# The rotation of the differential heads: from a permutation product on TensorE to eight 32-partition products on VectorE

## The chip, the cores and the metric

The kernel runs on one core of a Trainium2 chip. The metric is device time in microseconds (us) of one execution. The engines are called PE (TensorE, matrix products), DVE (VectorE), ACT (ScalarE), POOL (GpSimd) and SP (the engine that here only issues transfers).

## What is computed

The kernel computes a first block (RWKV mixer, convolution, feed-forward network) and a second block with two attention layers over 512 tokens and 256 context tokens. Only the second attention layer, with differential heads, is touched. It has 8 heads. Each has two queries and two keys of 64 dimensions, laid out on 128 partitions (dimension on the partition, token along the free axis). Queries and keys of the 512 tokens are rotated:

```python
def apply_rope(x, cos, sin):
    half = x.shape[-1] // 2
    x1 = x[..., :half].astype(jnp.float32)
    x2 = x[..., half:].astype(jnp.float32)
    return jnp.concatenate([x1 * cos - x2 * sin, x2 * cos + x1 * sin], axis=-1).astype(x.dtype)
...
        q = q.reshape(bsz, n, 2 * B_HEADS, B_HEAD)
        k = k.reshape(bsz, n, 2 * B_HEADS, B_HEAD)
        if rope:
            q = apply_rope(q, cos, sin)
            k = apply_rope(k, cos, sin)
```

So with 64 dimensions a half is 32: partitions 0 to 31 exchange with 32 to 63, and 64 to 95 with 96 to 127. Afterwards come the two softmaxes, their difference, the product with the values, a norm and a gate.

## The kernel before

Every engine has its own program, written out by hand; they meet at counting semaphores. The differential layer is a loop over heads. In iteration h, PE computes the projection of head h + 1 (four parts q, k, gate, v of eight chunks each, so 32 chunks c = 0 to 31, function `diff_chunk`, matrix products on L1390, L1391 and L1393) and puts the attention of head h between the chunks: scores u = 0 to 7 (`diff_scores`, L1425 and L1426) ahead of chunks 0, 3, ... 21, the transposes of the probabilities (`diff_turn`, L1433) ahead of chunks 8, 14, 20, 28, and the product with the values (`diff_values`, L1445) ahead of chunks 10, 16, 22, 30. PE executes its queue in order, so a wait in one of these holds everything behind it.

The rotation of head h + 1 in iteration h:

- ACT copies q and k from PSUM into `dq` (L1983) and `dk` (L1987).
- PE, ahead of chunk 19, multiplies both with a permutation matrix that also carries the signs (`diff_rotate`, L1400 and L1401), into PSUM.
- DVE multiplies the result with the sines (`read_rotated`, L2753 and L2754, into `dtq` and `dtk`), later `dq` and `dk` with the cosines (L2757, L2758) and adds (L2760, L2761), in `rope_sum`.
- ACT rounds to the high parts (`high_own`, `high_other`, L2007 to L2014), DVE takes the low parts (`low_parts`, L2765 to L2768). The scores of head h + 1 need both.

The order of DVE's queue in the last third of an iteration is fixed:

```python
            top(h, 6)
            read_rotated(h + 1)
            copy_turn(h, 2)
            rope_sum(h + 1)
            top(h, 7)
            mix(h, 3)
            out(h, 2)
            copy_turn(h, 3)
            low_parts(h + 1)
            out(h, 3)
```

`top` is the row maximum of a score (L2772), `mix` combines the two softmaxes (L2777 to L2781), `copy_turn(h, 2)` (L2787) copies half of the transposed probabilities out of PSUM, and `diff_values(h, 2)` on PE waits for it.

POOL splits each block of weights (1 MB, sixteen 128x128 tiles) into a high and a low part, eight instructions of 128x512 a block (L648 high, L639 low), two blocks a head. It may start on a block as soon as PE has finished with the buffer: after chunk 15 (the k part) and after chunk 31 (the v part). For head 0 the rotation stands outside the loop, between the chunks of head 0, and nothing of another head surrounds it; POOL also splits a block there.

Of the kernel before, what the change touches and what calls it, by code (L numbers as in the profile page):

```python
# [19 lines left out]
ALU = mybir.AluOpType  # L20
# [3 lines left out]
P = 128  # L24
T = 512
# [89 lines left out]
def build(nc, x_t, ctx_t, stream, ada_w, vectors, squares, level_masks, scan_mask, ropes, lora_w, gate_w,  # L115
# [10 lines left out]
    def fixed(name, shape, dt=F32, size=4):  # L126
        n = size
        for s in shape[1:]:
            n *= s
        t = at(name, shape, dt, place[0])  # L130
        place[0] += (n + 31) // 32 * 32
        return t
# [5 lines left out]
    sq_c = fixed("sq_c", [P, 8, P])  # L138
# [24 lines left out]
    sq = reg("sq", [P, KT, T], 16)  # L163
# [50 lines left out]
    pairs = [es.enter_context(nc.psum_tensor(f"banks{2 * i}{2 * i + 1}", [P, 2, 512], F32)) for i in range(4)]  # L214
# [6 lines left out]
    def sem(name):  # L221
        return es.enter_context(nc.semaphore(name))
# [42 lines left out]
    lora_in, lora_full, lora_evac = sem("lora_in"), sem("lora_full"), sem("lora_evac")  # L265
    chunk_end, exps_in, exps_done = sem("chunk_end"), sem("exps_in"), sem("exps_done")
    kk_raw, kk_sq, kk_sum, kk_max, kk_root = (sem(n) for n in ("kk_raw", "kk_sq", "kk_sum", "kk_max", "kk_root"))
# [109 lines left out]
    rope = at("rope", [P, 2, T], F32, tmp_at)  # L377
# [94 lines left out]
    dq = reg("dq", [P, T], 115)  # L472
    dk = reg("dk", [P, TA], 117)
# [4 lines left out]
    dtq = reg("dtq", [P, T], 135)  # L478
    dtk = at("dtk", [P, T], F32, tmp_at + 4 * KB)
# [11 lines left out]


    q_full = Later(lora_in, 2)
    rot_full = Later(lora_full, 12)
    gate_full = Later(lora_evac, 12)
    vt_full = Later(chunk_end, 1)
    q_evac = Later(exps_in, 2)
    k_evac = Later(exps_done, 4)
    gate_evac = Later(kk_raw, 4)
    v_evac = Later(kk_sq, 4)  # L500
    vt_evac = Later(kk_sum, 4)
    rot_read = Later(kk_max, 4)
    roped = Later(kk_root, 4)
    qk_high = Later(bonus_in, 4)
    qk_low = Later(bonus_sum, 4)
# [13 lines left out]
    X_PAIR, TURN, G_BANK, O_BANK = 1, (4, 5), 6, 7  # L519
# [199 lines left out]
    def _(pe):  # L719
        pe.wait_ge(one_done, 1)  # L720
        for k in range(KT):
            pe.wait_ge(sq_full, k + 1)
            for j in range(4):
                mm = pe.matmul(banks[7][:, j:j + 1], sq[:, k, P * j:P * j + P], der[:, ONE:ONE + 1], start=(k == 0 and j == 0),
                               stop=(k == KT - 1 and j == 3), skip_group_check=True)
# [199 lines left out]
        for n in range(NCH):  # L925
            tt, r = n // 2, slice(64 * (n % 2), 64 * (n % 2) + 64)
# [21 lines left out]
            for h in range(8):  # L948
                c, hr = h // 2, slice(64 * (h % 2), 64 * (h % 2) + 64)
# [10 lines left out]
            if n == 4:  # L960
                for c in range(CT):
                    pe.wait_ge(cln_sq, c + 1)
                    for j in range(4):
                        mm = pe.matmul(banks[5][32 * j:32 * j + 32, 0:P], ones[:, 0:32], csq[:, c, P * j:P * j + P], start=(c == 0),
                                       stop=(c == CT - 1))
# [44 lines left out]
        for c in range(CT):  # L1010
            rows = slice(32 * c, 32 * c + 32)
# [38 lines left out]
        with pe.Fori(0, 2) as i:  # L1050
            for u in range(6):
                s = half_of(STREAM["down"] + u)
                for t in range(TILES):
# [7 lines left out]
                    b = banks[4 + m]  # L1061
# [306 lines left out]
        def diff_chunk(h, part, k):  # L1368

            A, B = half_of(DIFF_A[h]), half_of(DIFF_A[h] + 1)  # L1370
            w, tile, wide_out = {"q": (A, k, False), "k": (A, KT + k, True), "gate": (B, k, False), "v": (B, KT + k, True)}[part]
            if k == 0:
                if part == "q":
                    pe.wait_ge(split_full, DIFF_A[h] + 1)
                    if h:
                        pe.wait_ge(*gate_evac.at(h))
                elif part == "k":
                    pe.wait_ge(*(vt_evac.at(h) if h else x_centred.at(KT)))
                elif part == "gate":
                    pe.wait_ge(split_full, DIFF_A[h] + 2)  # L1380
                    pe.wait_ge(*q_evac.at(h + 1))
                elif part == "v":
                    pe.wait_ge(*rot_read.at(h + 1))
            if h == 0 and part == "q":
                pe.wait_ge(mh_ready, KT + k + 1)
            hi, lo = w_hi[:, w, tile, :], w_lo[:, w, tile, :]
            own = key_pair(h) if part == "k" else X_PAIR
            spans = ((pairs[own][:, 0, :], 0, T), (pairs[own][:, 1, 0:C], T, TA)) if wide_out else ((banks[G_BANK][:, :], 0, T),)
            for out, a, b in spans:
                pe.matmul(out, hi, h2_hi[:, k, a:b], start=(k == 0), stop=False)  # L1390
                pe.matmul(out, hi, h2_lo[:, k, a:b], start=False, stop=False)  # L1391
            for out, a, b in spans:
                mm = pe.matmul(out, lo, h2_hi[:, k, a:b], start=False, stop=(k == KT - 1))  # L1393
            if k == KT - 1:
                mm.then_inc({"q": q_full.sem, "k": block_done, "gate": gate_full.sem, "v": block_done}[part], 1)

        def diff_rotate(h):
            pe.wait_ge(*q_evac.at(h + 1))
            pe.wait_ge(*k_evac.at(h + 1))
            pe.matmul(pairs[X_PAIR][:, 0, :], sq_c[:, 3, :], dq[:, :], start=True, stop=True)  # L1400
            pe.matmul(pairs[X_PAIR][:, 1, :], sq_c[:, 3, :], dk[:, 0:T], start=True, stop=True).then_inc(rot_full.sem, 1)  # L1401

        def diff_turn_v(h):
            pe.wait_ge(*v_evac.at(h + 1))
# [43 lines left out]
        PARTS = [(part, k) for part in ("q", "k", "gate", "v") for k in range(KT)]  # L1448
        TURN_AT, VALUES_AT = (8, 14, 20, 28), (10, 16, 22, 30)
        for c, (part, k) in enumerate([(part, k) for k in range(KT) for part in ("q", "k")] + PARTS[2 * KT:]):  # L1450
            if c == 19:
                diff_rotate(0)
            diff_chunk(0, part, k)
        for h in range(B_HEADS - 1):
            for c, (part, k) in enumerate(PARTS):
                if c % 3 == 0 and c < 24:
                    diff_scores(h, c // 3)
                if c == 2:
                    diff_turn_v(h)
                if c == 19:  # L1460
                    diff_rotate(h + 1)
                if c in TURN_AT:
                    diff_turn(h, TURN_AT.index(c))
                if c in VALUES_AT:
                    diff_values(h, VALUES_AT.index(c))
                diff_chunk(h + 1, part, k)
        h = B_HEADS - 1
# [660 lines left out]
    def _(dve):  # L2128
        chain = Chain(dve, dve_step)
# [196 lines left out]
        for n in range(NCH):  # L2326
            tt, r = n // 2, slice(64 * (n % 2), 64 * (n % 2) + 64)
# [113 lines left out]
        with conv.loop(N_UP // 2, 4) as i:  # L2441
            for u in range(2):
                s = half_of(STREAM["up"] + u)
                j = 2 * i + u
                for g, buf in enumerate((yg, yu)):
                    b = banks[2 * s + g]
# [45 lines left out]
        for e in range(2):  # L2492
            r, s = rope_rows(e), swap_rows(e)
# [4 lines left out]
        for e in range(2):  # L2498
            r = rope_rows(e)
# [24 lines left out]
        for e in range(2):  # L2524
            r = rope_rows(e)
# [61 lines left out]
        for e in range(2):  # L2587
            r = rope_rows(e)
# [160 lines left out]
        low_rows, high_rows = slice(0, 64), slice(64, 128)  # L2749

        def read_rotated(h):
            dve.wait_ge(*rot_full.at(h + 1))
            dve.tensor_tensor(dtq[:, :], pairs[X_PAIR][:, 0, :], rope[:, 1, :], ALU.mult)  # L2753
            dve.tensor_tensor(dtk[:, :], pairs[X_PAIR][:, 1, :], rope[:, 1, :], ALU.mult).then_inc(rot_read.sem, 1)  # L2754

        def rope_sum(h):
            dve.tensor_tensor(dq[:, :], dq[:, :], rope[:, 0, :], ALU.mult)  # L2757
            chain.link(dve.tensor_tensor(dk[:, 0:T], dk[:, 0:T], rope[:, 0, :], ALU.mult))  # L2758
            dve.wait_ge(*rot_read.at(h + 1))
            dve.tensor_tensor(dq[:, :], dq[:, :], dtq[:, :], ALU.add)  # L2760
            dve.tensor_tensor(dk[:, 0:T], dk[:, 0:T], dtk[:, :], ALU.add).then_inc(roped.sem, 1)  # L2761

# [65 lines left out]
        h = B_HEADS - 1  # L2828
# [38 lines left out]
        for t in range(4):  # L2867
            o = O_tok[:, t, P * h:P * h + P]
# [190 lines left out]
def constants():  # L3059

    j, t = np.meshgrid(np.arange(P), np.arange(P), indexing="ij")
    same = (j // CHUNK) == (t // CHUNK)
    sq = np.zeros((P, 9, P), np.float32)
    sq[:, 8] = (np.arange(P)[:, None] % 32 // 16 == np.arange(P)[None, :] // 64) / 16.0
    sq[:, 0] = j == t
    sq[:, 1] = 1
    sq[:, 2] = same
    sq[:, 4] = same & (j < t)
    sq[:, 5] = same & (j <= t)

    def rotation(rows, half):

        r = np.zeros((P, P), np.float32)
        for start in rows:
            for i in range(half):
                r[start + half + i, start + i] = -1
                r[start + i, start + half + i] = 1
        return r
    sq[:, 3] = rotation([0, 64], 32)
    lv = np.zeros((P, 12, P), np.float32)  # L3080
    for n in range(6):
        s = 1 << n
        low = (j // (2 * s) == t // (2 * s)) & (j % (2 * s) >= s) & (t % (2 * s) < s)
        lv[:, n] = low
        lv[:, 6 + n] = low.T
    scan = np.ones((P, T), np.float32)
    scan[:, ::CHUNK] = 0

    def angles(dim):
        n = dim // 4  # L3090
        inv = (np.float32(10000.0) ** (-np.arange(n, dtype=np.float32) / np.float32(n))).astype(np.float32)
        row, c = np.repeat(np.arange(T // 64, dtype=np.float32), 64), np.tile(np.arange(64, dtype=np.float32), T // 64)
        return np.concatenate([row[:, None] * inv, c[:, None] * inv], axis=-1).T
    ropes = np.zeros((2, P, 2, T), np.float32)
    a = angles(32)
    for o in (32, 48, 64, 80):
        ropes[0, o:o + 16, 0] = np.cos(a)
    for o in (0, 96):
        ropes[0, o:o + 16, 1], ropes[0, o + 16:o + 32, 1] = -np.sin(a), np.sin(a)
    b = angles(64)  # L3100
    for o in range(0, P, 32):
        ropes[1, o:o + 32, 0], ropes[1, o:o + 32, 1] = np.cos(b), np.sin(b)
    return {"squares": sq, "level_masks": lv, "scan_mask": scan, "ropes": ropes}


# [15 lines left out]
```

## Time and profile before

| quantity | value |
|---|---|
| median of 3 runs | 1777.9 us (1777.76 to 1782.23) |
| profiled execution, first to last instruction (its span) | 1776.4 us |
| PE busy | 1697.5 us (96%) |
| DVE busy | 1014.9 us (57%) |
| ACT busy | 763.0 us (43%) |
| POOL busy | 954.4 us (54%) |

For the profiled execution only the span is recorded; the median of the runs is 1.5 us above it. Busy time is what an engine's instructions took; a duration of a DVE or POOL instruction includes time in which it could not proceed. A row of the timeline gives the start, the duration, the engine and line, output<-inputs, the shapes, and in brackets the idle time of the engine before it with what ended it.

### The profile page before, as it was taken

Reading aid. Unit: us, or ns where it says so; the run is one execution under the profiler, and the core shown is the slowest. Engines: PE = TensorE matmul, PEld = TensorE weight load, DVE = VectorE, ACT = ScalarE, POOL = GpSimd, SP = SyncE. Lnnn points to the kernel's source line nnn. Section 1 sums busy time; section 2 is a strip of 40 time slices with the busy share of each in tenths; the row PEclk is TensorE's granted clock in tenths of the full one; section 3 lists DMA queues with packets and bytes.
Section 4 is the critical chain, followed back from the end, with each engine's and each line's share of the span. In section 5 each row is a group of like instructions: output and inputs, shape, how many; then the busy total and the mean of one; then the engine's idle time right before and its main releaser. Section 6 shows DMA issues by size and latency. Waiting matters only on the chain.

```text
span 1776.4 us, 26816 instructions
## 1 busy us (share of the span) xinstructions
PE 1697.5 (96%) x10602; PEld 1393.1 (78%) x10602; DVE 1014.9 (57%) x1276; ACT 763.0 (43%) x1261; POOL 954.4 (54%) x758
## 2 busy tenths in 40 slices
PE   8999999989799999999998999999989999999987
PEld 7677999867488888888787777776877888888765
DVE  4697544575655555201455666667485666666575
ACT  4553767422333333101433565567134444444572
POOL 4443777767099999999356022224554444444062
PEclk9999999989899999999999999999999999999998
DMA  5221000233022222424112000001331111111211
GB/s 191 72 95 48 2 1 2 97 145 157 33 75 101 102 100 94 166 101 170 50 48 72 25 24 1 25 0 57 110 155 48 48 47 44 45 45 46 88 68 48
DMA packets 18870, 126.38 MB, mean 71 GB/s; under 512 B 2096, under 2 KB 2352, under 8 KB 4304
## 3 DMA queue, kind: packets, MB, share of 16 engines
q1 hardware_dynamic: 18624, 124.41, 19.1%
q8 instruction: 75, 1.23, 0.3%
q10 hardware_dynamic: 144, 0.52, 0.1%
q14 instruction: 27, 0.22, 0.0%
HBM read 122.83 MB, written 2.10 MB: 70 GB/s over the span
## 4 chain that ended last, share of the span: by engine, by line
PE 51%; issue 19%; POOL 16%; DVE 9%; ACT 3%; DMA 0%; POOLq 0%; ACTq 0%; DVEq 0%; SPq 0%
POOL w_hi L648 8%; PE banks L1233 5%; POOL cacc L670 4%; PE banks L1212 4%; POOL w_lo L639 3%; PE banks L1390 3%; PE banks L1393 3%; PE banks L1391 3%; PE banks L1095 3%; PE banks L1100 3%; PE banks L1096 3%; PE banks L751 2%; PE banks L1445 2%; PE banks L752 2%; PE banks L753 2%
## 5 line engine op out<-in xcount | busy, mean ns | idle before, releaser
L648 POOL TENSOR_TENSOR w_hi<-raw,der 128x512 fp32r<-128x512 f32 x296 | 341.0, 1162 | 455.8 <-PE banks L1393 184.9
L639 POOL TENSOR_TENSOR w_lo<-raw,w_hi 128x512 fp32r<-128x512 f32 x336 | 468.9, 1408 | 65.9 <-ACT w_hi L1536 65.9
L751 PE MATMUL banks<-h_hi,w_hi 128*128 128x512 f32 x496 | 198.7, 401 | 5.6 <-DVE h_lo L2368 5.3
L752 PE MATMUL banks<-h_lo,w_hi 128*128 128x512 f32 x496 | 194.4, 392 | 0.0
L753 PE MATMUL banks<-h_hi,w_lo 128*128 128x512 f32 x496 | 194.2, 392 | 0.0
L1390 PE MATMUL banks<-h_hi,w_hi 128*128 128x512 f32 (+1 forms) x384 | 146.8, 382 | 0.1
L1391 PE MATMUL banks<-h_lo,w_hi 128*128 128x512 f32 (+1 forms) x384 | 131.5, 358 | 0.0
L2019 ACT ACTIVATE dP<-banks,der 128x768 f32<-128x768 f32 x64 | 57.7, 902 | 159.9 <-DVE der L2772 159.9
L751 PEld LDWEIGHTS banks<-h_hi,w_hi 128*128 128x128 f32 x496 | 93.6, 189 | 35.1 <-issue 12.7
L1393 PE MATMUL banks<-h_hi,w_lo 128*128 128x512 f32 (+1 forms) x384 | 116.5, 358 | 0.0
L698 POOL TENSOR_TENSOR Of<-Of,Ls 128x768 f32<-128x768 f32 x8 | 14.7, 1833 | 186.7 <-DVE Ls L2574 186.7
L752 PEld LDWEIGHTS banks<-h_lo,w_hi 128*128 128x128 f32 x496 | 93.8, 189 | 19.8 <-issue 1.4
L753 PEld LDWEIGHTS banks<-h_hi,w_lo 128*128 128x128 f32 x496 | 93.8, 189 | 19.5
L2772 DVE TENSOR_REDUCE der<-banks 128x1 f32<-128x768 f32 x64 | 60.8, 953 | 70.0 <-PE banks L1426 69.9
L1233 PE MATMUL banks<-Pf,V 128*128 128x512 f32 x192 | 99.2, 598 | 0.3 <-issue 0.3
L1095 PE MATMUL banks<-h_hi,w_hi 128*128 128x512 f32 (+1 forms) x256 | 92.6, 362 | 4.6 <-DVE h_lo L2471 1.8
L2563 DVE TENSOR_REDUCE nmr<-banks 128x1 fp32r<-128x768 f32 x64 | 60.5, 945 | 59.7 <-PE banks L1183 58.9
L670 POOL TENSOR_TENSOR cacc<-glu_s,cacc 128x512 f32<-128x512 f32 x48 | 60.3, 1278 | 63.7 <-ACT glu_s L1634 63.7
L1872 ACT ACTIVATE Pf<-banks 128x512 f32<-128x512 f32 x112 | 66.6, 595 | 62.8 <-PE banks L1212 60.8
L1096 PE MATMUL banks<-h_lo,w_hi 128*128 128x512 f32 (+1 forms) x256 | 86.1, 353 | 0.0
L1390 PEld LDWEIGHTS banks<-h_hi,w_hi 128*128 128x128 f32 x384 | 72.8, 190 | 16.4 <-issue 1.9
L1391 PEld LDWEIGHTS banks<-h_lo,w_hi 128*128 128x128 f32 x384 | 73.1, 190 | 10.3 <-issue 1.9
(491 smaller groups left out, 4152.5 us busy)
## 6 DMA issues: line engine op xcount, KB each, us to landing
raw<-in_stream SPq DMA_DIRECT2D x84, 1024.0 KB, 4.8
ada_raw<-in_ada_w SPq DMA_DIRECT2D x18, 1024.0 KB, 6.9
raw<-in_ada_w SPq DMA_DIRECT2D x4, 1024.0 KB, 4.8
xT<-in_x_t SPq DMA_DIRECT2D x2, 1024.0 KB, 6.1
xT<-in_x_t SPq DMA_DIRECT2D x1, 2048.0 KB, 7.9
ada_end<-in_ada_w SPq DMA_DIRECT2D x2, 1024.0 KB, 5.8
out_t<-z SPq DMA_DIRECT2D x8, 256.0 KB, 2.1
ctxT<-in_ctx_t SPq DMA_DIRECT2D x1, 1024.0 KB, 6.8
```

The costliest lines, as they stand in the source:

```text
L639: return pool.tensor_tensor(lo[:, h, part(i), :], raw_tiles(half)[:, part(i), :], hi[:, h, part(i), :], ALU.subtract)
L648: pool.tensor_tensor(hi[:, h, part(i), :], raw_tiles(half)[:, part(i), :], one, ALU.mult).then_inc(hi_done, 1)
L670: pool.tensor_tensor(cacc[:, j, :], tap_out[i % 4], cacc[:, j, :], ALU.add).then_inc(conv_done, 1)
L751: pe.matmul(banks[b][:, :], hi, tile(rhs_hi, k), start=(at_k == 0), stop=False)
L752: pe.matmul(banks[b][:, :], hi, tile(rhs_lo, k), start=False, stop=False)
L753: mm = pe.matmul(banks[b][:, :], lo, tile(rhs_hi, k), start=False, stop=(at_k == KT - 1))
L1095: pe.matmul(out, hi, cols(rhs_hi, k0 + k, a, b), start=(k == 0), stop=False)
L1096: pe.matmul(out, hi, cols(rhs_lo, k0 + k, a, b), start=False, stop=False)
L1233: mm = pe.matmul(pairs[1][:, 0, :], v[:, j, :], Pf[:, i % 4, :], start=(j == 0), stop=(j == 5), skip_group_check=True)
L1390: pe.matmul(out, hi, h2_hi[:, k, a:b], start=(k == 0), stop=False)
L1391: pe.matmul(out, hi, h2_lo[:, k, a:b], start=False, stop=False)
L1393: mm = pe.matmul(out, lo, h2_hi[:, k, a:b], start=False, stop=(k == KT - 1))
```

## The change

PE's permutation product goes away, with its semaphores. DVE reads the neighbouring half straight from `dq` and `dk` in SBUF: for each 32 partitions one product, input and sines at partitions r + 32, output at r, and the reverse; four for q and four for k, eight a head. The sign moves into the table of sines. `rope_sum` now begins with a wait until all eight are finished, and the v part of the projection (chunk 24) waits for the copy of k instead of the reading of the rotated product.

```diff
@@ PE @@
                 elif part == "v":
-                    pe.wait_ge(*rot_read.at(h + 1))
+                    pe.wait_ge(*k_evac.at(h + 1))
...
-        def diff_rotate(h):
-            pe.wait_ge(*q_evac.at(h + 1))
-            pe.wait_ge(*k_evac.at(h + 1))
-            pe.matmul(pairs[X_PAIR][:, 0, :], sq_c[:, 3, :], dq[:, :], start=True, stop=True)
-            pe.matmul(pairs[X_PAIR][:, 1, :], sq_c[:, 3, :], dk[:, 0:T], start=True, stop=True).then_inc(rot_full.sem, 1)
...
-            if c == 19:
-                diff_rotate(0)
...
-                if c == 19:
-                    diff_rotate(h + 1)
@@ DVE @@
         def read_rotated(h):
-            dve.wait_ge(*rot_full.at(h + 1))
-            dve.tensor_tensor(dtq[:, :], pairs[X_PAIR][:, 0, :], rope[:, 1, :], ALU.mult)
-            dve.tensor_tensor(dtk[:, :], pairs[X_PAIR][:, 1, :], rope[:, 1, :], ALU.mult).then_inc(rot_read.sem, 1)
+            for src, dst, done in ((dq, dtq, q_evac), (dk, dtk, k_evac)):
+                dve.wait_ge(*done.at(h + 1))
+                for r in range(0, P, 64):
+                    low, high = slice(r, r + 32), slice(r + 32, r + 64)
+                    chain.mark(dve.tensor_tensor(dst[low, :], src[high, 0:T], rope[high, 1, :], ALU.mult))
+                    chain.mark(dve.tensor_tensor(dst[high, :], src[low, 0:T], rope[low, 1, :], ALU.mult))
 
         def rope_sum(h):
+            chain.wait()
             dve.tensor_tensor(dq[:, :], dq[:, :], rope[:, 0, :], ALU.mult)
             chain.link(dve.tensor_tensor(dk[:, 0:T], dk[:, 0:T], rope[:, 0, :], ALU.mult))
-            dve.wait_ge(*rot_read.at(h + 1))
@@ the table of sines @@
-        ropes[1, o:o + 32, 0], ropes[1, o:o + 32, 1] = np.cos(b), np.sin(b)
+        ropes[1, o:o + 32, 0], ropes[1, o:o + 32, 1] = np.cos(b), -np.sin(b) if o % 64 else np.sin(b)
```

## Rows read from the trace of the kernel before

**Rows 1.** The page's first line.

```profile
span 1776.4 us, 26816 instructions
```

**Rows 2.** Busy time by engine in one iteration: us, busy by engine (instructions), granted clock.

```profile
1475.70:1520.40 44.70, 44.55 (x260) 37.72 (x259) 27.92 (x39) 18.97 (x40) 19.87 (x17) 1.00 0.14 48
```

**Rows 3.** Timeline of PE in one iteration, from chunk 19 on.

```profile
1478.14 1.02 PE L1400 MATMUL banks<-dq,sq_c 128*128 128x512 f32 x2
...
1480.09 0.39 PE L1391 MATMUL banks<-h_lo,w_hi 128*128 128x512 f32 x1
1480.32 0.39 PE L1393 MATMUL banks<-h_hi,w_lo 128*128 128x512 f32 x1
...
1483.29 1.50 PE L1445 MATMUL banks<-dV,dPT 128*128 128x128 f32 x12
...
1496.41 0.40 PE L1425 MATMUL banks<-KK,QQ 128*128 128x512 f32 x1
```

**Rows 4.** Timeline of DVE over the same rotation.

```profile
1478.56 0.94 DVE L2772 TENSOR_REDUCE der<-banks 128x1 f32<-128x768 f32 x1
1480.06 0.69 DVE L2753 TENSOR_TENSOR dtq<-banks,rope 128x512 f32<-128x512 f32 x1 [0.56 <-PE banks L1401]
...
1481.27 0.55 DVE L2787 COPY dPT<-banks 128x384 f32<-128x384 f32 x1
1481.73 1.58 DVE L2757 TENSOR_TENSOR dq<-dq,rope 128x512 f32<-128x512 f32 x1
1483.23 1.75 DVE L2758 TENSOR_TENSOR dk<-dk,rope 128x512 f32<-128x512 f32 x1
```

**Rows 5.** Timeline of POOL over the same rotation.

```profile
1479.23 1.27 POOL L639 TENSOR_TENSOR w_lo<-raw,w_hi 128x512 fp32r<-128x512 f32 x1
1480.46 1.04 POOL L648 TENSOR_TENSOR w_hi<-raw,der 128x512 fp32r<-128x512 f32 x1
1481.46 2.98 POOL L639 TENSOR_TENSOR w_lo<-raw,w_hi 128x512 fp32r<-128x512 f32 x2
```

**Rows 6.** Timeline of DVE: two low parts whose inputs and outputs start at other partitions.

```profile
1491.60 0.69 DVE L2765 TENSOR_TENSOR QQ<-dq,QQ 64x512 fp32r<-64x512 f32 x1 [0.28 <-ACT KK L2010]
1492.30 0.69 DVE L2766 TENSOR_TENSOR QQ<-dq,QQ 64x512 fp32r<-64x512 f32 x1
```

**Rows 7.** One line of the first attention layer: duration ns least/median/greatest, first and last start.

```profile
L2547 DVE TENSOR_TENSOR qf<-qf,otmp x16: 681/896/1336, 944.1 to 1203.0; 32x512 f32<-32x512 f32 x16
```

**Rows 8.** Timeline of the last iteration (rotation of head 7).

```profile
1656.53 0.96 DVE L2772 TENSOR_REDUCE der<-banks 128x1 f32<-128x768 f32 x1 [0.69 <-PE banks L1426]
...
1660.16 0.55 DVE L2787 COPY dPT<-banks 128x384 f32<-128x384 f32 x1
...
1662.19 1.50 PE L1445 MATMUL banks<-dV,dPT 128*128 128x128 f32 x12
...
1686.67 2.04 POOL L648 TENSOR_TENSOR w_hi<-raw,der 128x512 fp32r<-128x512 f32 x2 [46.13 <-DMA raw<-in_stream]
```

**Rows 9.** Timeline of the rotation of head 0, ahead of the loop.

```profile
1341.87 0.70 DVE L2795 MEMSET KL<- 64x768 f32 x1 [0.20 <-issue]
...
1342.91 2.04 POOL L648 TENSOR_TENSOR w_hi<-raw,der 128x512 fp32r<-128x512 f32 x2 [27.18 <-PE banks L1393]
...
1352.04 1.78 DVE L2761 TENSOR_TENSOR dk<-dk,dtk 128x512 f32<-128x512 f32 x1
...
1356.86 0.69 DVE L2765 TENSOR_TENSOR QQ<-dq,QQ 64x512 fp32r<-64x512 f32 x1 [3.05 <-ACT KK L2010]
...
1358.58 3.25 POOL L648 TENSOR_TENSOR w_hi<-raw,der 128x512 fp32r<-128x512 f32 x2 [5.32 <-PE banks L1393]
...
1361.18 0.47 PE L1425 MATMUL banks<-KK,QQ 128*128 128x512 f32 x1 [2.69 <-DVE KL L2768]
```

**Rows 10.** Two stretches of reduced granted clock: us, busy by engine, granted clock.

```profile
454.70:461.50 6.80, 4.61 (x6) 1.80 (x7) 6.80 (x12) 2.52 (x4) 0.00 (x0) 0.50 0.00 0
1362.60:1366.00 3.40, 3.40 (x12) 2.81 (x12) 0.52 (x1) 1.48 (x3) 3.40 (x4) 0.50 0.02 5
```

More of the change, by code:

```diff
@@ L493, in build @@
     q_full = Later(lora_in, 2)
-    rot_full = Later(lora_full, 12)
     gate_full = Later(lora_evac, 12)
@@ L501, in build @@
     vt_evac = Later(kk_sum, 4)
-    rot_read = Later(kk_max, 4)
     roped = Later(kk_root, 4)
@@ L3069, in constants @@
     sq[:, 5] = same & (j <= t)
[L3071 to L3079, printed above, removed]
     lv = np.zeros((P, 12, P), np.float32)
```

## The prediction

> **What bounds the kernel now.** I read the page first for the span [rows 1], then the busy time of one iteration of the head loop. An iteration takes 44.70 us and PE is busy for 44.55 of it, at full granted clock [rows 2]. So in the loop PE has practically no slack: what is taken off PE shortens it, and any wait on PE that wasn't there lengthens it. DVE is busy for 27.92 us and looks idle enough to take more work. But that is an average; the order of DVE's queue is fixed, so I read the timelines of PE, DVE and POOL side by side around the rotation. There the reader is to see three things: the copy L2787 stands directly behind the two products to be replaced, PE's product with the values follows it closely (copy finished at 1481.82, used at 1483.29), and POOL is splitting a block at that moment, while DVE's two SBUF products L2757 and L2758 take 1.58 and 1.75 us [rows 3 to 5].
>
> **What is removed from PE.** L1400 starts at 1478.14 where chunk 19 would start, and the second product of that chunk, L1391, starts at 1480.09. Consecutive products of a chunk are 0.23 us apart (1480.09, 1480.32). Without the rotation L1391 would start at 1478.37, so it costs 1480.09 - 1478.37 = 1.72 us a head, 13.8 us for 8 heads [rows 3]. This is the whole possible gain. The changed wait of chunk 24 costs nothing: the copy of k that it waits for lies ahead of the rotation already.
>
> **What is added to DVE.** Two products reading PSUM, 0.61 us each from start to start (1480.06 to 1481.27 for both, rows 4), make way for eight of 32 partitions reading SBUF twice. The trace of before has no such instruction, but close ones. With two SBUF inputs, 32x512, L2547 took 0.68 us at least and 1.34 at most, so 32 rows are neither cheaper than 128 nor free of the lengthening [rows 7]. When inputs and outputs change their first partition from one instruction to the next, starts are 0.70 us apart (1491.60, 1492.30) [rows 6]; the new ones change it every time, so I take 0.70 undisturbed. The lower bound is 0.61 (the PSUM products).
>
> Beside POOL they are longer. POOL's pair of L639 at 1481.46 takes 2.98 us where two alone take 2 x 1.27 = 2.54, and DVE's L2758 ends at 1484.98, 0.54 us after the pair (1484.44) [rows 4, 5]. Read together: the two engines take turns, one instruction each; DVE's ends about 0.55 us after POOL's, and each one put between lengthens POOL by 0.44 us.
>
> The Trainium skill (SBUF — State Buffer, "SBUF: two separate sides") says why: DVE instructions with two SBUF inputs and POOL instructions lock a common port pair for a whole instruction, and reading PSUM avoids that. The trace agrees (1.58 and 1.75 us here, 0.69 for L2753). By that rule alone the sum below would be the same; it speaks against the change, which turns PSUM readers into SBUF readers.
>
> **One iteration, h = 0 to 5.** `top(h, 6)` ends at 1479.50 [rows 4]. POOL is inside L639 until 1480.50 and has three instructions left (1.04, 1.27, 1.27) [rows 5].
>
> - Product 1 ends at 1480.50 + 0.55 = 1481.05.
> - POOL ends its next ones at 1480.46 + 0.44 + 1.04 = 1481.94, then + 0.44 + 1.27 = 1483.65, then 1485.36; products 2, 3 and 4 end at 1482.49, 1484.20 and 1485.91.
> - POOL is through; products 5 to 8 take 4 x 0.70: 1488.71. Then the copy, 0.55: 1489.3.
>
> PE can take up the product with the values at 1489.3. It would want it at 1483.29 - 1.72 = 1481.57, so it stands for 7.7 us, and against before it is 6.0 us late. Everything behind it in PE's queue is late too: ten chunks and the scores of the next head, 13.12 us later (1496.41 [rows 3]), now at 1502.4. Does a second wait follow? The low parts end near 1494.9 now (1491.60, two at 0.70 and two half again as long), 13.1 us after the copy, with 1.9 us of POOL's turns in it that are gone by then; that gives 1489.3 + 11.2 = 1500.5, before 1502.4. So it doesn't, by 1.9 us. POOL's own block ends about 1 us later, and before its next block it has more than ten us of rest (two blocks keep it busy 19.87 of 44.70 us, rows 2). 6 x 6.0 = 36 us.
>
> **The clock.** After a stall PE runs at half clock (1.2 for 2.4 GHz) for a while. After the 2.69 us stall at 1358.5 [rows 9] it was 0.50 for 3.40 us, all busy: 1.7 us lost. In the first layers a longer stall, ended at about 456.9, had 6.80 us of 0.50 around it, 4.61 of them busy: 2.3 us lost [rows 10]. For a stall of 7.7 us I take 2.0: 6 x 2.0 = 12 us. With none of it, 0; with all of 6.8 us busy, 3.4 a head.
>
> The Trainium skill (TensorE: Matmul & The Clock Gate, "Why this matters for your kernels") wants no gap above about 3 us to stay at full clock. Here 2.69 us was enough, so the row decides; by the page only the last head below could come out otherwise, by 1.7 us.
>
> **The last iteration, head 7.** POOL has nothing to do (idle for 46 us until 1686.67) [rows 8]. `top` ends at 1657.49, eight products make 1663.09, the copy 1663.65, against 1662.19 for the use before: 1.5 us late, a stall of 3.2, and 1.7 for the clock: 3.2 us.
>
> **Head 0.** Product 1 can start behind L2795 at 1342.6 and end at 1343.3. POOL then begins its block; products 2 to 8 take turns with seven of its eight instructions (7.97 us alone, and 6 x 0.44): the eighth ends near 1354.4, the sums near 1358.3 instead of 1353.82. ACT's 3.04 us of rounding bring the low parts to 1361.4 instead of 1356.86. PE is finished with its chunks 1.72 us earlier and releases POOL's next block (1358.58 before, about 1356.9 now), so all four low parts now take turns with it, some 1.0 us more for each of three or four: PE goes on near 1369 instead of 1361.18 [rows 9]. 8 us; bounds -5 (no turns at all, no stall) and 11.
>
> **Sum.** 36 + 12 + 3.2 + 8 = 59 us on the profiled execution's 1776.4, so 1835.6; the median lies 1.5 us above that span, so 1837 us, 3.3% slower.
>
> **Rivals.**
>
> 1. *The stall as above, but the clock isn't lowered, or far less.* For: PE has been dense for 30 us before it. Against: all of rows 10. 1837 - 12 - 2 = 1823. Chance 0.15.
> 2. *No turns with POOL*: 32 partitions don't wait, or POOL yields. Each copy then ends at 1479.50 + 8 x 0.70 + 0.55 = 1485.65, 2.4 us late, plus 1.7 for the clock: 7 x 4 = 28, less 5 for head 0: about 1800. With 0.61 for 0.70 and no clock loss, 1785. Against: 1.34 us of a 32x512 row [rows 7]. Chance 0.08.
> 3. *A second wait behind the first.* If the four sums or ACT's rounding come later than worked out, the 1.9 us of margin ahead of the next head's scores is used up; with the longer clock loss (3.4) as well, 10 to 11 us a head: 1777.9 + 6 x 10.5 + 3 + 11 = 1855. Chance 0.11.
> 4. *Not slower.* PE's 1.72 us is kept. This needs the copy L2787 by 1481.5, so eight products within 1.5 us of 1479.5, 0.19 us each, where no row is under 0.61; or DVE's `top(h, 6)` more than 4 us earlier. It decides at a product price of 0.19 us. Then 1777.9 - 13.8 = 1764. Chance 0.02, and 0.01 for within 0.3% (half of the gain eaten by head 0).
>
> My forecast has 0.63. The range reaches from near the second rival to the third: 1805 to 1852 us. Within 0.3% (5 us) is about what a measurement of this kernel can't tell from no change. Faster 0.02, same 0.01, slower 0.97.
>
> **What the profile will show.** Eight 32x512 products a head: the first four 1.4 to 1.8 us apart, the rest 0.70; L2787 of each third turn ending about 9.8 us after `top(h, 6)`; an idle time of 7 to 8 us on PE before L1445, released by DVE's copy, six times, and about 3 us a seventh time; after it a granted clock of 0.50 for some 3.4 us or more; an iteration of 52 to 53 us in place of 44.70; POOL's L639 in that stretch longer by 0.44. Before L1425 of head 0 PE idles some 12 us instead of 2.69. The prediction is wrong if the new products don't take turns with POOL, if PE's product with the values doesn't wait, or if DVE's order lets the copy go first.

## The result and the profile after

The changed kernel takes 1840.4 us (median of 4 runs, 1836.8 to 1848.7), the kernel before 1780.1 us in the same comparison: ratio 1.0349, 95% interval 1.0329 to 1.0370. It is slower by 3.5%; 1837 us and 3.3% were forecast. The profiled execution has a span of 1838.9 us against 1776.4.

The page's first lines for the changed kernel: span, busy time by engine, and the granted clock in 40 slices.

```profile
span 1838.9 us, 26784 instructions
...
PE 1708.5 (93%) x10570; PEld 1403.6 (76%) x10570; DVE 1064.3 (58%) x1324; ACT 763.4 (42%) x1261; POOL 963.6 (52%) x758
...
PEclk9999999999999999999999999999889899898998
```

PE's count is 32 lower than before (10602): each of the 16 products taken out is recorded as two instructions. Yet PE's busy time went up by 11 us: less work at a lower clock. Where, the last third of the slices (`PEclk`, tenths of the full clock) shows.

The timeline of DVE over one rotation in the loop of the changed kernel answers to [rows 4]:

```profile
1504.58 0.94 DVE L2763 TENSOR_REDUCE der<-banks 128x1 f32<-128x768 f32 x1
1505.55 1.53 DVE L2744 TENSOR_TENSOR dtq<-dq,rope 32x512 f32<-32x512 f32 x1
1507.11 1.42 DVE L2745 TENSOR_TENSOR dtq<-dq,rope 32x512 f32<-32x512 f32 x1
1508.56 1.64 DVE L2744 TENSOR_TENSOR dtq<-dq,rope 32x512 f32<-32x512 f32 x1
1510.23 1.64 DVE L2745 TENSOR_TENSOR dtq<-dq,rope 32x512 f32<-32x512 f32 x1
1511.90 0.68 DVE L2744 TENSOR_TENSOR dtk<-dk,rope 32x512 f32<-32x512 f32 x1
1512.61 0.68 DVE L2745 TENSOR_TENSOR dtk<-dk,rope 32x512 f32<-32x512 f32 x1
1513.33 0.69 DVE L2744 TENSOR_TENSOR dtk<-dk,rope 32x512 f32<-32x512 f32 x1
1514.04 0.68 DVE L2745 TENSOR_TENSOR dtk<-dk,rope 32x512 f32<-32x512 f32 x1
1514.76 0.56 DVE L2778 COPY dPT<-banks 128x384 f32<-128x384 f32 x1
```

The first four are lengthened, the other four are 0.71 us apart, and the copy ends at 1515.32, 9.8 us after `top(h, 6)` (1505.52). POOL's timeline beside it answers to [rows 5], and PE's to [rows 3]:

```profile
1505.26 1.28 POOL L637 TENSOR_TENSOR w_lo<-raw,w_hi 128x512 fp32r<-128x512 f32 x1
1506.50 1.49 POOL L646 TENSOR_TENSOR w_hi<-raw,der 128x512 fp32r<-128x512 f32 x1
1507.95 3.38 POOL L637 TENSOR_TENSOR w_lo<-raw,w_hi 128x512 fp32r<-128x512 f32 x2
```

```profile
1506.60 0.50 PE L1417 MATMUL banks<-KK,QQ 128*128 128x512 f32 x1 [0.22 <-ACT dP L2007]
...
1515.37 2.93 PE L1437 MATMUL banks<-dV,dPT 128*128 128x128 f32 x12 [7.09 <-DVE dPT L2778]
```

POOL's block ends at 1511.33, which is when the products become short. PE stood still for 7.09 us for the copy, and the twelve products with the values then took 2.93 us instead of 1.50 [rows 3], at a granted clock of 0.50. The waits of the whole stage name two new ones on PE and nothing else of size (us in total, times, longest):

```profile
PE banks L1437 <- DVE dPT L2778: 45.8, 7, 7.1
...
PE banks L1417 <- DVE KL L2759: 11.2, 1, 11.2
```

Two windows of the changed kernel (busy by engine, then the granted clock), each from the third low part of one head to that of the next, answer to [rows 2]:

```profile
1474.02:1526.47 52.45, 44.94 (x256) 38.28 (x255) 33.82 (x45) 19.00 (x40) 20.75 (x16) 0.93 0.11 41
1526.47:1579.86 53.39, 45.91 (x256) 39.01 (x255) 33.80 (x44) 19.00 (x40) 20.74 (x16) 0.90 0.11 40
```

Measured between the same marks (the third low part of a head, L2767 before, L2758 after), the 62.5 us between the two spans lie here: 1.8 us ahead of the rotation of head 0 (L2795 at 1341.87, its counterpart at 1343.67; nothing there was changed); 5.8 us in the rotation of head 0; 54.5 us from head 0's mark to head 7's (313.4 to 367.9 us); 0.4 us behind it.

### The profile page after: what moved, and what is told of

It is laid out like the page before. It is cut to its first block, busy times and chain, and to the rows that moved or that the text cites. A ratio compares the mean times of both kernels' runs of the same rounds, so it can differ in the third digit from the quotient of the medians.

```text
span 1838.9 us, 26784 instructions
## 1 busy us (share of the span) xinstructions
PE 1708.5 (93%) x10570; PEld 1403.6 (76%) x10570; DVE 1064.3 (58%) x1324; ACT 763.4 (42%) x1261; POOL 963.6 (52%) x758
## 4 chain that ended last, share of the span: by engine, by line
PE 47%; issue 19%; POOL 16%; DVE 14%; ACT 3%; DMA 0%; POOLq 0%; ACTq 0%; DVEq 0%; SPq 0%
POOL w_hi L646 8%; PE banks L1231 4%; POOL cacc L668 4%; PE banks L1210 3%; POOL w_lo L637 3%; PE banks L1093 3%; PE banks L1388 3%; PE banks L1391 3%; PE banks L1389 3%; PE banks L1098 3%; PE banks L1094 3%; PE banks L1437 2%; PE banks L749 2%; PE banks L750 2%; PE banks L751 2%
## 5 line engine op out<-in xcount | busy, mean ns | idle before, releaser
L646 POOL TENSOR_TENSOR w_hi<-raw,der 128x512 fp32r<-128x512 f32 x296 | 345.2, 1177 | 511.0 <-PE banks L1391 236.2
L637 POOL TENSOR_TENSOR w_lo<-raw,w_hi 128x512 fp32r<-128x512 f32 x336 | 474.5, 1425 | 67.0 <-ACT w_hi L1524 67.0
L1389 PE MATMUL banks<-h_lo,w_hi 128*128 128x512 f32 (+1 forms) x384 | 133.9, 363 | 0.0
L750 PEld LDWEIGHTS banks<-h_lo,w_hi 128*128 128x128 f32 x496 | 93.7, 189 | 19.9 <-issue 1.4
L1437 PE MATMUL banks<-dV,dPT 128*128 128x128 f32 x384 | 58.5, 311 | 50.3 <-DVE dPT L2778 47.4
L1437 PEld LDWEIGHTS banks<-dV,dPT 128*128 128x128 f32 x384 | 54.2, 222 | 54.8 <-DVE dPT L2778 50.8
L668 POOL TENSOR_TENSOR cacc<-glu_s,cacc 128x512 f32<-128x512 f32 x48 | 60.3, 1278 | 63.9 <-ACT glu_s L1622 63.9
```

The lines of the kernel that those rows point to most:

```text
L637: return pool.tensor_tensor(lo[:, h, part(i), :], raw_tiles(half)[:, part(i), :], hi[:, h, part(i), :], ALU.subtract)
L646: pool.tensor_tensor(hi[:, h, part(i), :], raw_tiles(half)[:, part(i), :], one, ALU.mult).then_inc(hi_done, 1)
L668: pool.tensor_tensor(cacc[:, j, :], tap_out[i % 4], cacc[:, j, :], ALU.add).then_inc(conv_done, 1)
L750: pe.matmul(banks[b][:, :], hi, tile(rhs_lo, k), start=False, stop=False)
L1437: mm = pe.matmul(banks[O_BANK][:, 0:P], dPT[:, kt, :], dV[:, kt, :], start=(kt == 0), stop=(kt == 5))
```

## The experiments

All were compared with the kernel before in runs on the same chip. The first five change the changed kernel in one point each.

**PE's permutation kept.** Its result is read by nobody.

```diff
...
+            if c == 19:
+                diff_rotate(0)
...
+                if c == 19:
+                    diff_rotate(h + 1)
...
         def rope_sum(h):
             chain.wait()
+            dve.wait_ge(*rot_full.at(h + 1))
```

> The changed kernel, with the permutation products of PE put back (their result is read by nobody; the sums wait for them). Theory (the loop is set by DVE's eight products ahead of the copy, PE's 1.72 us a head merely shortens work that then stands still): the iterations of the loop keep their 52.9 us, PE's stall before the product with the values falls from 7.1 to about 5.4 us, and the time is that of the changed kernel within 4 us (about 1840). Rival (the gain of 13.8 us is real and only outweighed by a loss elsewhere): the time rises by 10 to 14 us, to about 1852.

Measured: 1842.3 us, ratio 1.0335 (1.0301 to 1.0370); the changed kernel's is 1.0349, so no difference. One iteration, to be held against the second window above:

```profile
1475.19:1528.68 53.49, 47.42 (x260) 39.89 (x259) 33.81 (x44) 19.12 (x40) 20.77 (x16) 0.94 0.11 40
```

PE is busy for 1.5 us more in an iteration of the same length (53.49 and 53.39), and the stall is shorter:

```profile
1516.51 2.93 PE L1444 MATMUL banks<-dV,dPT 128*128 128x128 f32 x12 [5.90 <-DVE dPT L2790]
```

5.90 instead of 7.09 us, where about 5.4 had been expected; the 0.22 us of wait ahead of a score, seen in the changed kernel, are gone as well. What was taken off PE only made it wait longer.

**The copy first.**

```diff
+            copy_turn(h, 2)
             read_rotated(h + 1)
-            copy_turn(h, 2)
             rope_sum(h + 1)
```

> The changed kernel with one line moved: the copy of the transposed probabilities (third turn) stands ahead of the eight products on DVE. Theory (a wait on the order of DVE's queue): the stall of 7.1 us before the product with the values goes away, but the eight products now delay the last score's maximum and with it the fourth turn: PE idles 5 to 6.5 us there, an iteration takes 50 to 52 us, total about 1825 to 1832. Rival (only the copy mattered): no new stall, iterations of 43 us, total about 1773.

Measured: 1830.2 us, ratio 1.0264 (1.0234 to 1.0295). The stall moved, as the theory has it:

```profile
1520.11 1.54 PE L1425 MATMUL banks<-sq_c,Pd 128*128 128x128 f32 x6 [5.67 <-DVE Pd L2772]
```

PE now stands still for 5.67 us ahead of the fourth turn, because the combination L2772 is behind `top(h, 7)`, which is behind the products. Iterations take 51.2 to 51.7 us but for the first (52.6) and the last. Moving one instruction out of the way isn't enough: 9 us of work in a queue delays whatever comes next in it.

**POOL nearly idle.** POOL splits 8 of the 128 columns of each tile for heads 1 to 7 (high and low parts), so these are computed with mostly old weights.

```diff
...
+            cols = slice(0, 8) if light else slice(0, P)
...
-                pool.tensor_tensor(hi[:, h, part(i), :], raw_tiles(half)[:, part(i), :], one, ALU.mult).then_inc(hi_done, 1)
+                pool.tensor_tensor(hi[:, h, part(i), cols], raw_tiles(half)[:, part(i), cols], one[:, :, cols], ALU.mult).then_inc(hi_done, 1)
```

> The changed kernel, in which POOL splits only 8 of 128 columns of each tile for the weights of heads 1 to 7, so that it takes little time (those heads are computed with old weights). Theory (the first four products of an iteration cost 1.5 us instead of 0.70 because they take turns with POOL): all eight products 0.68 to 0.72 us apart, the stall before the product with the values 3.2 us as in the last iteration, head 0 without its long wait, total about 1795 (-45 against the changed kernel). Rival (32-partition products are dear for a reason of their own, such as the starting partitions): the first four stay at 1.4 to 1.7 us, total within 10 us of 1840.

Measured: 1798.9 us, ratio 1.0087 (1.0053 to 1.0122). The first of each two q products in the whole run (least, median, greatest duration in ns), and PE's waits for the copy:

```profile
L2746 DVE TENSOR_TENSOR dtq<-dq,rope x16: 680/684/687, 1349.6 to 1677.0; 32x512 f32<-32x512 f32 x16
...
PE banks L1439 <- DVE dPT L2780: 24.3, 9, 3.2
```

In the changed kernel the same product (there L2744) goes from 680 to 1642 ns with a median of 1528. The same instruction at the same partitions is short once POOL is out of the way, so neither the 32 partitions nor the starting partitions lengthen it. The stall is 3.2 us seven times, head 0 has almost none (0.8 us), an iteration takes 47.5 us. Of the 60 us, some 42 go with POOL's work, and 17 remain: eight products in front of the copy are too many even at 0.71 us each.

**PE kept at work.** 26 products that nobody reads fill the stall.

```diff
+            if qt == 2 and h < B_HEADS - 1:
+                pe.wait_ge(*o_done.at(n))
+                for _ in range(26):
+                    pe.matmul(banks[O_BANK][:, :], w_hi[:, half_of(DIFF_A[h + 1] + 1), 0, :], h2_hi[:, 0, 0:T], start=True, stop=True)
             pe.wait_ge(*eva_done.at(n + 1))
```

> The changed kernel with 26 products of 128x512 put on PE ahead of the wait of the third product with the values (six us of work that nobody reads, in the place of the 7.1 us stall). Theory (the stall of 7.1 us costs a further 2 us a head because PE then runs at 1.2 GHz): granted clock 1.00 through the loop, iterations of 50.7 to 51.3 us instead of 52.9, total 1825 to 1830. Rival (the clock is not what makes the iterations longer than 50.7 us): total unchanged or higher, 1840 to 1845.

Measured: 1827.3 us, ratio 1.0268 (1.0237 to 1.0300): 13 us less than the changed kernel, with more work. One iteration, and PE across the filled stall:

```profile
1467.12:1518.07 50.95, 49.34 (x282) 41.66 (x281) 33.89 (x45) 18.88 (x40) 20.82 (x16) 1.00 0.12 42
```

```profile
1501.19 6.09 PE L1436 MATMUL banks<-h_hi,w_hi 128*128 128x512 f32 x26
1508.53 1.60 PE L1441 MATMUL banks<-dV,dPT 128*128 128x128 f32 x12 [1.25 <-DVE dPT L2782]
```

Full clock, 50.9 us against a mean of 53.0 in the changed kernel (the five iterations between the first and the last): the lowered clock costs 2.1 us an iteration. From head 0's mark to head 7's the profile is 11.4 us shorter (356.5 for 367.9 us); the last iteration is 0.8 us longer, because there the 26 products take longer than the stall that they fill.

**Two products instead of eight.** The same tiles in SBUF, each partition with itself; the halves are not exchanged.

```diff
-                for r in range(0, P, 64):
-                    low, high = slice(r, r + 32), slice(r + 32, r + 64)
-                    chain.mark(dve.tensor_tensor(dst[low, :], src[high, 0:T], rope[high, 1, :], ALU.mult))
-                    chain.mark(dve.tensor_tensor(dst[high, :], src[low, 0:T], rope[low, 1, :], ALU.mult))
+                chain.mark(dve.tensor_tensor(dst[:, :], src[:, 0:T], rope[:, 1, :], ALU.mult))
```

> The changed kernel with two products of 128 partitions in the place of the eight of 32, reading the same tiles in SBUF (each partition with itself, so the halves are not exchanged). PE's permutation is gone, DVE has no more instructions than before, only its two inputs are both in SBUF. Theory (each SBUF product beside POOL costs 1.5 instead of 0.61 us): the copy ends 1.3 us later than before, the product with the values is taken up about when it was before, with a stall near 1.5 us, an iteration takes 44.4 to 44.7 us, total within 4 us of before (1778 to 1784). Rival (it is the number of products alone): iterations of 43.0 us, total 13 us under before.

Measured: 1780.1 us, ratio 1.0001 (0.9981 to 1.0022). As many DVE instructions as before, no permutation on PE, and no gain:

```profile
1479.23 1.64 DVE L2742 TENSOR_TENSOR dtq<-dq,rope 128x512 f32<-128x512 f32 x1
1480.80 1.52 DVE L2742 TENSOR_TENSOR dtk<-dk,rope 128x512 f32<-128x512 f32 x1
1482.24 0.54 DVE L2775 COPY dPT<-banks 128x384 f32<-128x384 f32 x1
```

PE stands still for the copy and once more ahead of the fourth turn, and is busy for 43.60 us of an iteration:

```profile
1482.84 1.61 PE L1437 MATMUL banks<-dV,dPT 128*128 128x128 f32 x12 [0.78 <-DVE dPT L2775]
...
1490.46 0.87 PE L1425 MATMUL banks<-sq_c,Pd 128*128 128x128 f32 x6 [0.43 <-DVE Pd L2769]
```

Iterations take 45.19 us, 0.5 above the upper end of what was expected (44.4 to 44.7), although the stall ahead of the product with the values is 0.78 and not 1.5 us. With the number of DVE instructions unchanged, moving their source from PSUM to SBUF at this place gives back all that PE saved.

**The products spread.** All eight are kept. Two of q stand where POOL rests, two more behind `top(h, 4)`, the four of k read the projection in PSUM behind the copy, and `top(h, 7)` goes ahead of the sums. PE's v part waits until k has been read.

```diff
...
             out(h, 0)
+            rotated_q(h + 1, 0)
             top(h, 4)
+            rotated_q(h + 1, 64)
             copy_turn(h, 1)
...
-            read_rotated(h + 1)
             copy_turn(h, 2)
-            rope_sum(h + 1)
+            rotated_k(h + 1)
             top(h, 7)
+            rope_sum(h + 1)
```

> The changed kernel with the same eight products spread: two of q behind the first output of an iteration, two behind the maximum of score 4 (POOL rests there), the four of k read PSUM instead of SBUF and stand behind the copy, and the maximum of score 7 goes ahead of the sums. Theory (the loss is only where the products stand and that they take turns with POOL): no stall on PE in the loop, all eight at 0.70 us, an iteration takes 43.0 us, full clock; head 0 still takes turns with POOL for its q products and costs about 5 us. Total 1768 to 1776, 0.3 to 0.7% under before. Rival (eight products are too many for DVE's queue anywhere): scores wait for ACT or DVE elsewhere and iterations take 45 us or more.

Measured: 1774.4 us against 1781.2, ratio 0.9962 (0.9944 to 0.9981): 0.4% under the kernel before and 3.6% under the changed one. The k products and POOL beside them:

```profile
1482.00 0.68 DVE L2743 TENSOR_TENSOR dtk<-banks,rope 32x512 f32<-32x512 f32 x1
1482.71 0.68 DVE L2744 TENSOR_TENSOR dtk<-banks,rope 32x512 f32<-32x512 f32 x1
```

```profile
1481.24 1.28 POOL L638 TENSOR_TENSOR w_lo<-raw,w_hi 128x512 fp32r<-128x512 f32 x1
1482.48 1.03 POOL L647 TENSOR_TENSOR w_hi<-raw,der 128x512 fp32r<-128x512 f32 x1
```

Neither is lengthened by the other. An iteration takes 43.5 us, not the 43.0 expected; PE is busy for 43.1 of it and waits twice for 0.2 us, for ACT ahead of a score and for DVE ahead of a turn.

**The same with k from SBUF.**

```diff
...
-            chain.mark(rotated(dtk, wide(key_pair(h)), 0))
-            rotated(dtk, wide(key_pair(h)), 64).then_inc(rot_read.sem, 1)
+            chain.mark(rotated(dtk, dk, 0))
+            rotated(dtk, dk, 64).then_inc(rot_read.sem, 1)
```

> As the spread kernel, but the four products of k read SBUF. Theory (only SBUF inputs take turns with POOL): those four take 1.4 to 1.7 us each, the combination ahead of the fourth turn is 2 to 3 us later, PE idles about 2 us ahead of that turn, an iteration takes 45 to 47 us, total 1783 to 1800. Rival (POOL doesn't matter at this place): same as the spread kernel.

Measured: 1791.0 us, ratio 1.0051 (1.0031 to 1.0070). Same place, same shape, same neighbours:

```profile
1491.98 1.06 DVE L2742 TENSOR_TENSOR dtk<-dk,rope 32x512 f32<-32x512 f32 x1
1493.08 1.42 DVE L2743 TENSOR_TENSOR dtk<-dk,rope 32x512 f32<-32x512 f32 x1
1494.53 1.65 DVE L2742 TENSOR_TENSOR dtk<-dk,rope 32x512 f32<-32x512 f32 x1
1496.21 1.67 DVE L2743 TENSOR_TENSOR dtk<-dk,rope 32x512 f32<-32x512 f32 x1
```

Four iterations take 45.5 us and one 47.1 (the first and the last aside); PE waits 1.8 us ahead of the fourth turn in each of the first six. In the long iteration the granted clock fell behind this wait (0.61 over the 4.4 us after it), in the others it stayed at 1.00. In head 0 POOL lengthens seven of the eight products again, and the stall ahead of the first score is 11.2 us; in the spread kernel POOL lengthens three, and the stall is 4.1 us.

This kernel has all eight products of the changed one, all reading SBUF; beside the order of DVE's queue only one wait, of DVE for its own product, is new. So the order alone brings 1840.4 down to 1791.0 us, and the source of k this to 1774.4.

**Head 0 with the permutation.** The spread kernel, but head 0 rotated by PE as before.

```diff
...
+            if c == 19:
+                diff_rotate(0)
...
-        rotated_q(0, 0)
-        rotated_q(0, 64)
-        rotated_k(0)
+        dve.wait_ge(*rot_full.at(1))
+        chain.mark(dve.tensor_tensor(dtq[:, :], pairs[X_PAIR][:, 0, :], rope[:, 1, :], ALU.mult))
+        dve.tensor_tensor(dtk[:, :], pairs[X_PAIR][:, 1, :], rope[:, 1, :], ALU.mult).then_inc(rot_read.sem, 1)
...
+    sq[:, 3] = -1.0 * (j == (t ^ 32))
```

> The spread kernel with head 0 rotated by PE's permutation product as before (both entries of the matrix negative, to go with the new table of sines). Theory (head 0 costs time because nothing hides its products and they take turns with POOL): PE's wait ahead of the first score is 2.7 to 4.5 us as before, iterations 43.0 us, total 1764 to 1769, about 12 us under before and 4 to 7 under the spread kernel. Rival (head 0 costs nothing): the same as the spread kernel.

Measured: 1773.1 us, ratio 0.9962 (0.9943 to 0.9981). Against the spread kernel this is no difference that can be told, though the stall ahead of the first score is 2.7 instead of 4.1 us and the iteration behind it 42.6 instead of 45.7 us. The total lies some 4 us above the 1764 to 1769 expected.

## Why the prediction was right, point by point

- *What is removed* (1.72 us a head). This was somewhat too much. With the permutation kept, PE's busy time in an iteration rises by 1.5 us (45.91 to 47.42) and the time stays, so in the changed kernel the term is worth nothing, as predicted. Where PE sets the pace, in the spread kernels, PE is busy for 1.5 us less than before (43.09 for 44.55) and the iteration is 44.7 - 43.5 = 1.2 us shorter; the difference is two waits of 0.2 us each, where before PE was idle for 0.15 us in all.
- *Eight products, turns with POOL.* 9.8 us from `top(h, 6)` to the end of the copy, forecast 9.8. Products 1 to 4 at 1.4 to 1.7 us, the rest at 0.71. That POOL is the cause is shown twice: by the light POOL (0.68 us throughout) and by the pair of spread kernels, in which the PSUM readers take 0.68 us and the SBUF readers up to 1.67 at the same place. The rule of the Trainium skill (SBUF — State Buffer, "SBUF: two separate sides") about the port pair shared by DVE instructions with two SBUF inputs and POOL agrees in both directions: the inputs' place decides, not the size.
- *The stall.* 7.09 us and 0.22 ahead of a score before it, forecast 7.7; the removal that was put too high is part of the difference. Without the clock's part an iteration is 50.9 - 44.7 = 6.2 us longer (forecast 6.0). No second wait came behind it, as worked out: the low parts end at 1528.38 and the next head's scores start at 1530.13, a margin of 1.75 us for the 1.9 forecast.
- *The clock.* Forecast 2.0 us an iteration, measured 2.1 by keeping PE at work (53.0 against 50.9). The first rival, no loss of clock, is out. But the 2.0 was a choice between rows, and no iteration lost just that: the iterations take 52.4 and 53.4 us in turn, so they lose 1.5 and 2.5 us, and that the mean fits is in part luck. The two kinds differ in how long PE works at 1.2 GHz behind the stall, 3.23 or 5.52 us (busy by engine, then the granted clock; the stalls end at 1515.37 and 1461.88):

```profile
1515.37:1518.60 3.23, 3.23 (x14) 3.13 (x15) 3.19 (x5) 0.00 (x0) 0.00 (x0) 0.50 0.02 8
1461.88:1467.40 5.52, 5.52 (x19) 4.94 (x20) 4.36 (x8) 0.99 (x3) 0.00 (x0) 0.50 0.01 3
```

  The stall of 3.21 us in the last iteration lowered it too:

```profile
1722.59 2.19 PE L1437 MATMUL banks<-dV,dPT 128*128 128x128 f32 x12 [3.21 <-DVE dPT L2778]
```

  The iteration is 3.6 us longer than before (48.05 for 44.49), forecast 3.2.
- *Head 0.* A stall of 11.17 us ahead of the first score, forecast 12 (2.69 before [rows 9]):

```profile
1369.72 0.77 PE L1417 MATMUL banks<-KK,QQ 128*128 128x512 f32 x1 [11.17 <-DVE KL L2759]
```

  PE goes on 8.5 us later than before (1369.72 for 1361.18), 1.8 of which were there already: 6.7 us for the 8 forecast. The miss is in the low parts: the four took 6.0 us instead of 4.1, so 1.9 more, where three to four were forecast. On the other side the clock's part behind the stall was left out of the sum: PE then worked for 5.58 us at half clock, before for 3.40 [rows 10], which makes 1.1 us. The two misses nearly cancel (7.8 for 8), and that is luck.
- *The sum.* 59 us forecast, 62.5 between the two spans, 60.3 between the medians. Of the 62.5, 1.8 lie ahead of anything that was changed. The stretch from mark to mark took 54.5 us more, and 51.2 were forecast for the loop. But head 0's mark stands ahead of the moment at which PE goes on, so 1.0 of head 0's own 6.7 us and its 1.1 us of clock fall into that stretch; the loop itself is then about 52.4, and some 1.2 us short in the forecast.
- *The rivals.* No turns with POOL: the light POOL shows what that world looks like, 1799 us for the forecast 1800. That the two agree is chance in part: 1800 was worked out from 28 us in the loop less 5 for head 0, while from mark to mark the light POOL costs 15.6 us (329.0 for 313.4) and ahead of head 0's mark it gains nothing. A second wait: in the changed kernel no other one of PE in the loop is longer than 0.2 us; one appears, ahead of the fourth turn, when the copy is moved ahead (5.67 us). Not slower: would have needed products of 0.19 us.

That the order of DVE's queue and not DVE's load is the trouble is shown by the spread kernels: with the eight products in other places and all reading SBUF 49 of the 60 us go, and in an iteration of the kernel with head 0 permuted, DVE is busy for 30.24 of 43.49 us, more than the 27.92 of before [rows 2], and the time is lower.

```profile
1445.39:1488.88 43.49, 43.09 (x256) 36.88 (x255) 30.24 (x44) 19.10 (x40) 19.42 (x16) 1.00 0.14 49
```

What stays open is why the two best kernels hardly differ in their totals. In their profiles the one with head 0 permuted is 4.6 us ahead at head 7's mark (1662.38 for 1666.97), as expected, but the stretch behind it took 107.3 us and in the other 105.6, which hides 1.7 us; whether it does so in each run wasn't tried.

## What to carry to other kernels

An engine that is 60% busy is no free place: look at what stands behind the new instructions in its queue and at who waits for that, and place them where neither is pressed. Eight products a head cost 60 us in one place, 10 in others, and nothing once the four that POOL still held up read PSUM. Before moving an operand from PSUM to SBUF on DVE, look at what POOL does at that moment, and price a stall on PE with the clock that it loses.

## What the runs showed of the hardware

- DVE and POOL take turns, one instruction each, and both pay: POOL's L646 went from 1.04 to 1.49 us and the pair of L637 from 2.98 (with one DVE product between, [rows 5]) to 3.38. In these runs it met DVE instructions with both inputs in SBUF; beside a busy POOL the 32-partition products that read PSUM kept their 0.68 us and the copy out of PSUM its 0.54.
- The loss of clock behind equal stalls wasn't equal. Iterations alternated between 52.4 and 53.4 us with the same 7.09 us of stall; the granted clock averaged 0.93 and 0.90. Shorter stalls lowered the clock in some cases only: with the light POOL six of seven stalls of 3.2 us were followed by a stretch at half clock and the seventh was not (granted clock 1.00 over the 6 us behind it), and of six waits of 1.8 us in the spread kernel with k from SBUF one was.
- A stretch of lowered clock need not come from the edit. Ahead of the rotation of head 0, in code that is the same in both, PE stood still for 2.0 us in either kernel; the changed kernel then ran for 14 us at a granted clock of 0.51, with PE busy nearly throughout, while the kernel before had 0.88 over the same 14 us. The profiles of the other kernels fall on both sides as well: 0.51 with head 0 permuted, 0.88 in the spread kernel. The row is the changed kernel's:

```profile
1307.00:1321.00 14.00, 13.78 (x177) 12.09 (x179) 10.66 (x18) 1.83 (x4) 7.24 (x6) 0.51 0.78 308
```

  So a difference of 2 us ahead of an edit, between single profiles of two kernels, says nothing.
